# Two edits to a transformer layer on one core: attention with values stationary and scores two tiles ahead, and norms tile by tile

## The reference

```python
h = rms_norm(x, g_mix)
p, q, k, v, gate_pool, gate_attn = split(h @ w_in)        # 512, 512, 128, 128, 1024, 1024
q, k = partial_rope(q), partial_rope(k)                   # 8 query heads and 2 key heads of 64
yA = pool_mixer(p) @ w_branch_pool                        # trailing means over 2, 4, 8, 16 tokens
yB = window_attention(q, k, v, sinks) @ w_branch_attn     # chunks of 64: own and previous chunk, a sink per head
x = x + (sigmoid(gate_pool) * yA + sigmoid(gate_attn) * yB) @ w_out
x = x + peer(rms_norm(x, g_ffn))                          # 8 heads, 16 of 128 x 128 experts each
return rms_norm(x, g_final)
```

## Time and profile before

| | |
|---|---|
| Median of 3 executions | 3024.1 us (3023.41 to 3024.41) |
| The profiled execution's own time | 3019.19 us |
| Its span, first to last instruction | 3017.4 us |
| TensorE busy | 2844.6 us, 94% |
| VectorE busy | 2336.3 us, 77% |
| GpSimd busy | 2124.3 us, 70% |
| ScalarE busy | 937.1 us, 31% |
| Mean granted TensorE clock | 0.972 |

### The profile page before, as it was taken

One profiled execution on the slowest core, in us unless ns is written; L12 is line 12 of the kernel. 1 busy time (PEld: TensorE's weight loads), 2 busy tenths in 40 slices (PEclk: granted clock), 3 DMA queues, 4 the chain that ended last, 5 costly groups with the idle time before them and its releaser, 6 DMA issues.

```text
span 3017.4 us, 40171 instructions
## 1 busy us (share of the span) xinstructions
PE 2844.6 (94%) x15235; PEld 2477.6 (82%) x15235; DVE 2336.3 (77%) x4348; ACT 937.1 (31%) x1356; POOL 2124.3 (70%) x1552
## 2 busy tenths in 40 slices
PE   7999898999899799899999998999999989999996
PEld 6678777677689688889998997899899979989995
DVE  1332298345499899588999999898899979889998
ACT  4232433232332399322222222222222222222221
POOL 4324576338568799778887886888688868878883
PEclk9899999899899899999999999999999999999998
DMA  3112412112322377989998997999899979989996
GB/s 140 43 63 91 168 64 70 42 50 98 112 87 94 120 238 237 332 310 330 347 349 315 342 336 289 335 342 341 311 343 336 346 266 339 348 311 341 335 337 219
DMA packets 267584, 717.92 MB, mean 238 GB/s; under 512 B 20864, under 2 KB 104064, under 8 KB 267392
## 3 DMA queue, kind: packets, MB, share of 16 engines
q0 software_dynamic: 110912, 403.75, 35.8%
q1 hardware_dynamic: 156480, 311.61, 30.6%
HBM read 657.86 MB, written 57.41 MB: 237 GB/s over the span
## 4 chain that ended last, share of the span: by engine, by line
PE 34%; DVE 8%; POOL 7%; DMA 6%; issue 3%; ACT 1%; DVEq 0%; SPq 0%; ACTq 0%
PE abank L1530 6%; PE abank L1532 6%; PE abank L1531 6%; PE ybank L1546 6%; PE ybank L1547 5%; PE ybank L1548 5%; POOL up L1475 3%; DVE acc L1684 3%; DMA up<-in_down,e_idx 3%; POOL tdown_lo L1482 2%; DMA up<-in_up,e_idx 2%; DVE up L1672 2%; DVE e_y L1731 1%; POOL tup_lo L1486 1%; DMA w<-all_pre 1%
## 5 line engine op out<-in xcount | busy, mean ns | idle before, releaser
L1530 PE MATMUL abank<-m_hT,tdown_hi 128*128 128x384 f32 (+1 forms) x1856 | 576.4, 311 | 15.0 <-ACT w L1588 9.0
L817 POOL TENSOR_TENSOR m_wlo<-m_raw,m_whi 128x1024 fp32r<-128x1024 f32 x128 | 309.5, 2425 | 379.9 <-ACT m_whi L622 376.7
L1532 PE MATMUL abank<-m_hT,tdown_lo 128*128 128x384 f32 (+1 forms) x1856 | 575.9, 310 | 0.0
L1531 PE MATMUL abank<-m_hlo,tdown_hi 128*128 128x384 f32 (+1 forms) x1856 | 574.9, 310 | 0.0
L1546 PE MATMUL ybank<-tup_hi,w_hi 128*128 128x512 f32 x1280 | 509.1, 398 | 45.5 <-DVE e_y L1731 32.7
L1684 DVE SCALAR_TENSOR_TENSOR acc<-up,e_act,acc 128x1024 f32<-128x1024 f32 x381 | 489.7, 1285 | 65.9 <-DMA up<-in_up,e_idx 43.4
L1672 DVE CUSTOM_DVE_ANT_0 up<-up,acc 128x1024 f32<-128x1024 f32 x384 | 457.0, 1215 | 97.8 <-DMA up<-in_down,e_idx 95.2
L1547 PE MATMUL ybank<-tup_lo,w_hi 128*128 128x512 f32 x1280 | 506.2, 396 | 0.0
L1548 PE MATMUL ybank<-tup_hi,w_lo 128*128 128x512 f32 x1280 | 504.2, 394 | 0.0
L1475 POOL DMA_INDIRECT up<-in_up,e_idx x384 | 396.9, 1033 | 106.0 <-issue 92.4
L1475 POOL DMA_INDIRECT up<-in_down,e_idx x384 | 399.1, 1039 | 99.3 <-issue 88.9
(11 more groups left out here) (226 smaller groups left out, 4714.6 us busy)
## 6 DMA issues: line engine op xcount, KB each, us to landing
e_tup<-in_up SPq DMA_DIRECT2D x128, 512.0 KB
m_raw<-in_tiles SPq DMA_DIRECT2D x116, 512.0 KB, 3.3
e_tdown<-in_downT SPq DMA_DIRECT2D x116, 512.0 KB
gates<-all_table SPq DMA_DIRECT2D x64, 640.0 KB
all_table<-t_out SPq DMA_DIRECT2D x9, 4096.0 KB, 14.7
m_raw<-in_downT SPq DMA_DIRECT2D x12, 512.0 KB, 3.7
up<-in_down,e_idx POOLq DMA_INDIRECT x384
up<-in_up,e_idx POOLq DMA_INDIRECT x384
```

Source lines behind the costliest of these rows:

```text
L1530: nc.tensor.matmul(out, tdown_hi[:, q, at], h2T_hi[:, k, a:b], start=k == 0, stop=False)
L1531: nc.tensor.matmul(out, tdown_hi[:, q, at], h2T_lo[:, a:b, at], start=False, stop=False)
L1532: ins = nc.tensor.matmul(out, tdown_lo[:, q, at], h2T_hi[:, k, a:b], start=False, stop=k == KD - 1)
```

## The change

Two edits are made together.

**Attention.** (1) v is projected like the others; ACT keeps it in `q4[:, 3]`, PE transposes it in four matmuls behind the first q tile. (2) The values are the stationary factor: per tile four fp32 matmuls of 512 columns, for each of the two key heads and each of two key tiles, written to partitions 0 to 63 and 64 to 127. The result stands as the branch needs it, so `ya` and its transposes go; the rows of `w_branch_attn` are reordered on the host. (3) The shares are divided by their sums before the transposes (`shares` on DVE, SBUF to SBUF, 4 heads at a time). (4) A second probability buffer `pr_odd`, and scores two tiles ahead: gate projection, scores of tiles 0 and 1, gate projection; then per tile transposes, group matmul, values, scores of tile t + 2, gate projection. (5) The mask is loaded apart, copied by ACT to fp32r, and its matmul is one in fp32r. (6) POOL's pooled means stand one or two weight tiles later.

**Norms.** Roots are taken by the tile (`ROOTS`; at the start by two), and the tiles are scaled by the engines that `SCALES` names; PE's transposes wait tile by tile (`turn_normed`). A small root (`sqrt_soon`) brings the table load forward. For group 1, ACT scales behind each of the last four query tiles into other buffers (`junk`). The output projection keeps `k` outermost for its first five weight tiles; the last three are run so that token tiles 0 and 1 end first, then 2, then 3. In the first group POOL makes a weight tile's low part between the two halves of a choice instead of only ahead of both.

```diff
+ROOTS = {norm: ((0,), (1,), (2,), (3,)) for norm in NORMS}
+ROOTS[0, 0] = ((0, 1), (2, 3))
+ROOTS[1, 0] = ((0, 1, 2, 3),)
+SCALES = {norm: ("dve", "dve", "act", "both") for norm in NORMS}
+SCALES[0, 0] = ("dve", "pool", "act", "dve")
+SCALES[1, 0] = ("act", "act", "act", "act")
...
+SPLIT_OUT = KD - RING
...
+        pr_odd = [place("pr_odd0", [P, NH // 2, 2 * P], F32, at_h + 4 * TT * D), place("pr_odd1", [P, NH // 2, 2 * P], F32, at_rope)]
...
+        def pr_of(t, kv):
+            return pr_odd[kv][:] if t % 2 else pr[:, 4 * kv:4 * kv + 4]
+
+        def scaled_place(g, n, t):
+            return junk[t][:] if (g, n) == (1, 0) else h[:, t]
...
+            sp.dma_start(mask_in_f32[:], io["mask"]).then_inc(mask_in, 16)
...
-                pe.wait_ge(h_ready, g * 2 * TT + TT)
-                for k in range(KD):
-                    turn(("xT", k), [h[:, t, k * P:(k + 1) * P] for t in range(TT)])
+                def turn_normed(name, n):
+
+                    for t in range(TT):
+                        wait_scaled(pe, g, n, t)
+                        for k in range(KD):
+                            out = begin(name, k) if t == 0 else bank(name, k)
+                            ins = nc.tensor.transpose(out[:, t * P:(t + 1) * P], scaled_place(g, n, t)[:, k * P:(k + 1) * P], ident)
+                            if t == TT - 1:
+                                ins.then_inc(job_full, 1)
+
+                turn_normed("xT", 0)
...
-                out = begin("v")
-                w_hi, w_lo = weights("v")
-                for t in range(TT):
-                    for k in range(KD):
-                        at = slice(k * P, (k + 1) * P)
-                        ins = term(out[:, t * P:(t + 1) * P], hT[:, k, t], hlo[:, t, at], w_hi[:, at], w_lo[:, at],
-                                   k == 0, k == KD - 1)
-                ins.then_inc(job_full, 1)
+                project(("v",), ("v",))
...
+                    if j == 0:
+                        pe.wait_ge(vT_kept, g + 1)
+                        turn(("vT",), [q4[:, 3, t * P:(t + 1) * P] for t in range(TT)])
...
-                    mask = const[:, C_MASK:C_MASK + 2 * WK] if t == 0 and g == 0 else const[:, C_MASK + 2 * WK:C_MASK + 4 * WK]
+                            pe.wait_ge(mask_ready, 1)
+                    unseen = mask[:, P:P + 2 * WK] if t == 0 and g == 0 else mask[:, P + 2 * WK:]
...
-                        nc.tensor.matmul(out[:, 0:2 * WK], const[:, C_ROWS:C_ROWS + P], mask, start=True, stop=False)
+                        nc.tensor.matmul(out[:, 0:2 * WK], mask[:, 0:P], unseen, start=True, stop=False)
...
+                project(EARLY[0], EARLY[0])
                 scores(0)
+                scores(1)
+                project(EARLY[1], EARLY[1])
                 for t in range(TT):
                     for i in range(4):
-                        pe.wait_ge(exp_ready, g * 9 * TT + 9 * t + 2 * i + 2)
-                        turn(("pT", t, i), [pr[:, 2 * i + e // 2, (e % 2) * P:(e % 2 + 1) * P] for e in range(4)])
-                    if t + 1 < TT:
-                        scores(t + 1)
-                    project(EARLY[t], EARLY[t])
-                    out = begin("pv", t)
-                    pe.wait_ge(prT_ready, g * 4 * TT + 4 * t + 4)
-                    if t == 0:
-                        pe.wait_ge(v_ready, g + 1)
-                    for hd in range(NH):
-                        kv, at = slice(hd // 4 * HD, (hd // 4 + 1) * HD), slice(hd * HD, (hd + 1) * HD)
-                        nc.tensor.matmul(out[:, at], prT[:, 2 * hd], v[:, t, kv], start=True, stop=False)
-                        ins = nc.tensor.matmul(out[:, at], prT[:, 2 * hd + 1], v[:, t + 1, kv],
-                                               start=False, stop=True)
-                    ins.then_inc(job_full, 1)
+                        kv, e = i // 2, i % 2
+                        pe.wait_ge(pr_ready, 2 * (g * TT + t) + kv + 1)
+                        turn(("pT", t, i), [pr_of(t, kv)[:, j, e * P:(e + 1) * P] for j in range(4)])
...
-                    pe.wait_ge(ya_ready, g * TT + t + 1)
-                    turn(("yaT", t), [ya[:, j * P:(j + 1) * P] for j in range(4)])
+                    out = begin("pv", t)
+                    pe.wait_ge(prT_ready, g * 4 * TT + 4 * t + 4)
+                    if t == 0:
+                        pe.wait_ge(v_ready, g + 1)
+                    for kv in range(2):
+                        for e in range(2):
+                            ins = nc.tensor.matmul(out[kv * HD:(kv + 1) * HD], v[:, t + e, kv * HD:(kv + 1) * HD],
+                                                   prT[:, 8 * kv + 4 * e:8 * kv + 4 * e + 4].rearrange("p j c -> p (j c)"),
+                                                   start=e == 0, stop=e == 1)
+                    ins.then_inc(job_full, 1)
+                    if t + 2 < TT:
+                        scores(t + 2)
+                        project(EARLY[t + 2], EARLY[t + 2])
...
+                for k in range(SPLIT_OUT):
+                    weights("out", k)
                     pe.wait_ge(m_low, g * KD + k + 1)
-                    for t, n in outs:
-                        out = begin("xo", t, n) if k == 0 else bank("xo", t, n)
-                        ts, ds = slice(t * P, (t + 1) * P), slice(n * 512, (n + 1) * 512)
-                        ins = term(out[:], mhi(k)[:, ts], mlo[:, k, ts], w_hi[:, ds], w_lo[:, ds], k == 0, k == KD - 1)
+                    for t in range(TT):
+                        for n in range(2):
+                            ins = out_term(k, t, n)
+                    ins.then_inc(out_used, 1)
+                pe.wait_ge(m_low, g * KD + KD)
+                for of, ks in (((0, 1), range(SPLIT_OUT, KD - 1)), ((0, 1), (KD - 1,)), ((2,), range(SPLIT_OUT, KD))):
+                    weights("out", ks[-1])
+                    for t in of:
+                        for n in range(2):
+                            for k in ks:
+                                ins = out_term(k, t, n)
+                            if k == KD - 1:
+                                ins.then_inc(job_full, 1)
+                for k in range(SPLIT_OUT, KD):
+                    for n in range(2):
+                        ins = out_term(k, TT - 1, n)
                         if k == KD - 1:
                             ins.then_inc(job_full, 1)
                     if k < KD - 1:
                         ins.then_inc(out_used, 1)
...
-                pe.wait_ge(h_ready, g * 2 * TT + 2 * TT)
-                for k in range(KD):
-                    turn(("xT2", k), [h[:, t, k * P:(k + 1) * P] for t in range(TT)])
+                turn_normed("xT2", 1)
...
+                nc.scalar.activation(small[:, 20:21], of, ACT.Sqrt, scale=0.0)
...
+            act.wait_ge(x_in[0], 16)
+            sqrt_soon(x[:, 0, 0:1])
+            for of in ROOTS[0, 0]:
+                for t in of:
+                    act.wait_ge(x_in[t], 16)
+                    ins = squares(t, h[:, t])
+                ins.then_inc(ssq_ready, 1)
+                root(0, 0, of)
+            scaled(0, 0, 2)
...
+            act.wait_ge(mask_in, 16)
+            nc.scalar.activation(mask[:], mask_in_f32[:], ACT.Copy).then_inc(mask_ready, 1)
...
+                nc.scalar.activation(q4[:, 3], bank("v")[:], ACT.Copy).then_inc(vT_kept, 1)
...
                     act.wait_ge(m_ready, g * TT + t + 1)
-                    if t:
-                        wait_job(act, g, "pT", t - 1, 3)
                     if t > 1:
-                        act.wait_ge(ya_ready, g * TT + t - 1)
+                        wait_job(act, g, "pT", t - 2, 3)
+                        act.wait_ge(pr_ready, 2 * (g * TT + t - 1))
                     if t == 0 and g:
                         act.wait_ge(zeroed, 2)
+                    if t == 1:
+                        act.wait_ge(pad_zeroed, g + 1)
+                    nc.scalar.activation(es[t % 2], sarg, ACT.Exp).then_inc(exp_ready, 1)
...
+                def keep_early(t):
...
+                keep_early(0)
+                expon(0)
+                expon(1)
+                keep_early(1)
+                for t in range(TT):
...
-                    wait_job(act, g, "yaT", t)
+                    wait_job(act, g, "pv", t)
                     nc.scalar.activation(yaT[:, :, t * P:(t + 1) * P],
-                                         bank("yaT", t)[:].rearrange("p (j c) -> p j c", j=4), ACT.Copy).then_inc(yaT_ready, 1)
+                                         bank("pv", t)[:].rearrange("p (j c) -> p j c", j=4), ACT.Copy).then_inc(yaT_ready, 1)
+                    if t + 2 < TT:
+                        expon(t + 2)
+                        keep_early(t + 2)
...
+                sqrt_soon(vecs[:, 0:1])
                 for t in range(TT):
                     act.wait_ge(x2_ready, g * 2 * TT + 2 * t + 2)
-                    ins = squares(t, h[:, t])
-                ins.then_inc(ssq_ready, 1)
-                after("out", KD - 1)
```

(80 more changed lines are left out.)

172 lines of the change are left out of this document (97 added, 75 removed).

## The result

The changed kernel takes 2958.97 us (median of 4 runs, 2957.57 to 2964.01) against 3024.26 (4 runs); the ratio is 0.9784, interval 0.9772 to 0.9796. Five more runs in another session gave 2959.61 and 0.9786. The forecast was 2978, range 2963 to 2996: the direction was right, the gain was 65 us where 46 were forecast. The profiled execution took 2957.76, its span is 2956.0, 61.4 us under that of before.

The account below looks back on a forecast made before the run. PE was taken to bound the attention and branch stages, DVE's top-16 search the windows behind. Terms of -17.2 -16.6 -9.2 -4.5 -1.5 +5.4 -2.4 sum to -46.0, taking the median 3024.1 to 2978 us; range 2963 to 2996.

Parts of the forecast that it names:

- values stationary: Attention: four fp32 matmuls replace sixteen, 4.08 us per tile against 3.51, plus 2.3 us per half.
- Rival 2: Value matmuls writing different partition halves overlap: 8 us more gain, 2970, or 2964 with a cheap norm; chance 0.14.
- The mask: Attention scores: mask matmul in one fp32r pass, taken as 0.25 us each, minus 9.6 us per half.
- Waits and clock in attention: First half: old waits minus 5.6 and 1.0, full clock minus 5.9 and 1.7, new waits plus 0.6 and 5.7 us.
- Start: Kernel start: tiles scaled by three engines in two halves, first projection ending near 24.1 instead of 28.8; minus 4.5 us.
- v: Projection of v done like the others plus four transposes instead of 96 small matmuls; minus 4.6 us, twice.
- between the halves: Scaling earlier into other buffers starts the residual at 468.5: minus 2.9, cold PE plus 0.5 us.
- second output projection: Weights' low part late behind a POOL choice: wait of 4.7 and 1.7 of clock, net plus 5.4 us.
- Norm behind the output projection: Tile-by-tile norm after E, the output projection's end: 0.6 and 0.9 saved, minus 1.5 us; bounds -4 and +4.
- The reordered low parts on POOL: First search: they remove PE's waits at 431 and 455, which DVE hides; gain nothing.
- The expert stage: Stage from 1240 on, not edited: what the mixer gains should pass through whole.

Follow-up runs that it names:

- e_wide: Changed kernel with value matmuls taking all 128 columns of v as stationary instead of one key head's 64; 2973.95 us.
- e_forms: Changed kernel with another form of value matmuls in each of tiles 0 to 2: halves alternating, pairs repeated, 96 stationary columns; 2971.92 us, one execution.
- e_mask32: Changed kernel with the mask's tile float32 again, so its matmuls take two passes instead of one; 2973.78 us.
- e_gate_late: Changed kernel with the first gate's projection moved from ahead of the scores to behind the scores of tiles 0 and 1; 2980.78 us.
- v_pool: Changed kernel with POOL making all low parts of the second half's output weights before its last two choices of the first half; 2949.24 us.
- v_store: Changed kernel with SP issuing the stores of x2 one tile earlier, before the load of the search's fifth query tile; 2954.76 us.
- e_norm: The change's norm part alone, with attention and projection v as in the kernel before; 3023.55 us.
- e_attn: The change's attention part alone, with norms, output projection's order and choices as in the kernel before; 2968.38 us.

## Why the prediction was too low

- **The step that failed** is "values stationary: four fp32 matmuls of 512 columns ... 1.02 ..., so 4.08: plus 0.57 x 4". Two things were wrong in it. A matmul alone shows 1.02, in a row one costs 0.88 (e_wide). And passes in different column halves run in pairs: 1.87 us to the next instruction, against 3.51 of the sixteen old ones (e_forms shows the pairing, e_wide what is lost without it, 1.53 us per tile). Measured the term is -1.64 x 4 = -6.6 in place of +2.3: 8.9 us per half, 18 in all, where the forecast missed the median by 19 and its range by 4. Rival 2 named the mechanism, but counted one overlapping step of four instead of all, so even its 2970 was too high. Its "against" (all matmuls here start one after another) was no evidence: no two neighbours in the old trace wrote different halves.
- **The mask** was mis-sized the other way: 0.37 instead of 0.25, -7.7 instead of -9.6; e_mask32 confirms it by its 15 us.
- **Waits and clock in attention** held: the scores began without a wait at full clock, tile 3 waited 2.69 us of 2.9 forecast, its transposes took 3.25 instead of 1.9, and the waits ahead of the value matmuls were 0.45 to 0.50 per tile, not 0.2; e_gate_late puts 8.7 us per half on the cover of the first wait. Tile 3 after:

```profile
139.51 3.25 PE L518 MATMUL bank<-m_const,m_pr_odd 128*128 128x128 f32 x16 [2.69 <-DVE m_pr_odd L1242]
```

- **Start, v, between the halves, second output projection**: right within 1 us each, the last with the very wait forecast (4.65 of 4.7). v_pool shows its cause, and that it took the 3.49 us wait, which before had too, with it.
- **Norm behind the output projection** was worth 8.2 us and not 1.5. DVE scales half a tile in 0.49 us where 1.29 was priced for a whole one from an operation of the expert stage. That row was no like case: it writes its result (`acc`) to PSUM, the memory of the banks, the norm's to SBUF. So the last tile was scaled 7.2 us behind E and not 9, and the next projection began 10.9 and 10.6 behind E and not 12.9; in the second half it also ran at full clock, in the first not:

```profile
308.62 0.49 DVE L1089 TENSOR_SCALAR m_h<-m_x,m_small 128x512 f32<-128x512 f32 x1
```

- **"The reordered low parts on POOL ...: nothing"** was wrong by 4.6 us. I followed POOL's order, not SP's: the stores of x2 wait in SP's queue, as v_store shows.
- So the norm part pays back to POOL's and SP's queues nearly all that it gains: 13.8 us gained and 11.9 lost in e_norm. Between the halves e_attn too gains 1.6 us beyond those of v, so of the 3.1 only about half comes from the norm part.
- The expert stage gave 2.5 us back in the profile, hardly more than the 2.3 by which two profiles of the kernel after differ there. The median of the runs lay 5.1 us above the profiled one before and 1.2 after, which is the rest of the 65.

## What to carry to other kernels

Where a matmul uses 64 columns or 64 rows of the array, put its neighbour into the other half: the column halves paired here within one bank, the row halves were tried in two banks only, and that reordering of the scores gave 8 us. Where a neighbour fills more than its half, nothing is paired (96 columns). Price a matmul by start to start in a row of its like, not by one that stands alone. When a stage is made earlier, follow every queue (here SP's stores and POOL's choices) to the first instruction that now stands in front of something wanted sooner: two such moves were worth 15 us (4.9 and 10.4) after a norm change that alone was worth nothing.

## What was not expected of the hardware

- Passes in different column halves run in pairs even with three passes of the lower half between them in the program (the kernel after; e_forms, tile 1).
- The same for halves of the rows: eight passes of 192 columns in 0.92 us, where four took 0.91.
- DVE multiplied 1024 columns by a scalar per partition in 0.75 us in the norm, from SBUF to SBUF, and in 1.29 us in the expert stage, where the result goes to PSUM. No run here tests whether that is the cause:

```profile
295.74 0.75 DVE L1089 TENSOR_SCALAR m_h<-m_x,m_small 128x1024 f32<-128x1024 f32 x1
```
